# Storing a product's left matrix in column pairs, with one fewer place for gathered rows

## The chip, the cores and the metric

The kernel runs on one core of a Trainium2 chip. The metric is the device time of one execution in microseconds (us). Engines: PE is TensorE, DVE is VectorE, ACT is ScalarE, POOL is GpSimd, and SP only issues transfers here.

## The reference, cut to what matters

The program is two transformer-like blocks on 256 tokens of width 2048. The change touches the end of the second block, a layer in which every token picks 128 of 16384 experts:

```python
def block(args):                     # xt: 128 tokens, it: their 128 expert numbers, gt: weights
    xt, it, gt = args
    u = jnp.take(expert_u, it, axis=0)
    act = jax.nn.gelu(jnp.einsum('td,tkd->tk', xt, u)) * gt
    v = jnp.take(expert_v, it, axis=0)
    return jnp.einsum('tk,tkd->td', act, v)
```

The two blocks of 128 tokens are called t = 0 and t = 1. After this layer comes a residual sum and a final RMS norm.

## The kernel before

All engines walk one list of items that `Plan` writes; each engine executes, in the list's order, the items that it has a function for. The change concerns the last stage, which `dense` (from L1098) lists and which follows after everything else.

For the *lower* 1024 columns of the result, the rows of `expert_v` are not gathered. Before the stage, the activations of each token are scattered into a matrix over all 16384 experts, `A` (two halves, one for each t, in one tensor `AA`), built in 64 groups: PE makes a group in PSUM banks T0 or T1 (`build`, L1937), ACT copies it to SBUF (`keep_group`, L2426). The stage then multiplies `A` with the whole table: 128 tiles of 128 experts by 1024 columns. For tile j:

- SP copies the tile from HBM into `Vr` (L1609, 512 KB, five buffers, NT = 5). The copy for tile j waits until PE has finished tile j - 5.
- ACT rounds it to `Vh` (`high`, L2440, three buffers), and in the same function copies the tile's 2 x 128 columns of `AA` rounded into `Ah` (L2446, two buffers; the buffer is free when PE has finished tile j - 2).
- DVE makes the remainders, `Vl` in `low` (L3091) and `Al` in `low_a` (L3098).
- PE (`mul`, L1941) multiplies high by high, high by low and low by high in a fast format: 12 products of 512 columns, summed in the four banks W over all tiles. In 16 of the 128 tiles, those with j % 8 == 3, nothing is split: ACT copies the columns to `Ar`, and PE multiplies `Ar` and `Vr` whole.

For the *upper* 1024 columns the rows are gathered. Those of t = 0 were done earlier. Those of t = 1 (128), and 32 lower halves of t = 1 that the matrix leaves out, are the 160 *asides*: POOL gathers 128 half rows (512 KB) into one of five places `side` (L3224, NA = 5), and DVE multiplies by the activation and adds to `X` (`aside`, L3113). A gather into a place waits for the aside that used it before, NA earlier. Each aside on DVE also waits for the one ahead of it.

The order within a tile comes from `dense`: `high`, `low`, then one or two asides (160 over 120 tiles), then `low_a`, then `mul`. Four products on PE (`gain`, L1982) stand after tiles 7, 11, 15 and 19; at tile 22 ACT and DVE have a piece of the final norm (`upper`). DVE and ACT each take their instructions strictly in order, so whatever stands behind a waiting one waits too.

```python
a = 0
for j in range(128):
    self.add("high", j)
    self.add("low", j)
    if j == 0:
        self.add("rows")
    while a < min(ASIDES, (j - 1) * ASIDES // 120):
        self.add("aside", a)
        a += 1
    self.add("low_a", j)
    self.add("mul", j)
```

Of the kernel before, what the change touches and what calls it, by code (L numbers as in the profile page):

```python
# [7 lines left out]
F32 = mybir.dt.float32  # L8
F32R = mybir.dt.float32r
U32 = mybir.dt.uint32  # L10
ALU = mybir.AluOpType
ACT = mybir.ActivationFunctionType
AX = mybir.AxisListType.X
ADD, SUB, MUL = ALU.add, ALU.subtract, ALU.mult

P = 128
# [16 lines left out]
HALF = D // 2  # L33
# [4 lines left out]
FIRST_ROWS = 102  # L38
NT = 5
NH = 3  # L40
NA = 5
ASIDES = 128 + LATE
RAW = 8
NX = 5
U_SETS = ((48, (0, 1, 2, 3)), (190, (0, 1, 2, 3, 4, 5)), (218, (0, 2, 3, 4, 5)), (256, (2, 3, 4, 5)))
BACKLOG = {"ACT": 3.0, "DVE": 4.5, "DMA": 1e9}
# [104 lines left out]
def landings():  # L151

    count, table = [0] * NE, {}
    for kind, n, place in ("row", 128, row_sem), ("aside", ASIDES, lambda i: i % NA):
        for i in range(n):
# [22 lines left out]


def whole_tile(j):  # L180
    return j % RAW == 3


SPLIT_TILES = [j for j in range(128) if not whole_tile(j)]


def aside_of(i):
# [107 lines left out]
class Plan:  # L295
# [801 lines left out]
    def dense(self):  # L1097

        for i in range(ASIDES):
            self.add("get_aside", i)  # L1100
        a = 0
        for j in range(128):
            self.add("high", j)
            self.add("low", j)
            if j == 0:
                self.add("rows")
            while a < min(ASIDES, (j - 1) * ASIDES // 120):
                self.add("aside", a)
                a += 1
            self.add("low_a", j)  # L1110
            self.add("mul", j)
            if j % 4 == 3 and 7 <= j <= 19:
                self.add("gain", (j - 7) // 4)
            if j == 22:
                self.add("upper", 0)
        self.add("upper", 1)
        self.add("close")
# [77 lines left out]
def strided(a, *dims):  # L1195
    return bass.AP(tensor=a.tensor, offset=a.offset, ap=[list(a.ap[0])] + [list(d) for d in dims])


def program(nc, io, out):
    plan = Plan()  # L1200
    blocks, subs, chunks = plan.blocks, plan.subs, plan.chunks
    with ExitStack() as ctx:
        def sem(name):
            return ctx.enter_context(nc.semaphore(name))
# [3 lines left out]
        def at(name, shape, offset, dt=F32):  # L1208
            return nc.alloc_sbuf_tensor_at(name, [P] + list(shape), dt, offset=offset)
# [6 lines left out]
        class Area:  # L1216
# [17 lines left out]
        keep = low("keep", [2, T])  # L1234
# [22 lines left out]
        u0 = top[0]  # L1257
# [99 lines left out]
        A0_o, A1_o = 65280, 163808  # L1357
        AA = at("AA", [(END - A0_o) // 4], A0_o)
        A = [AA[:, o:o + P * P].rearrange("p (g k) -> p g k", k=4 * P) for o in (0, (A1_o - A0_o) // 4)]
# [39 lines left out]
        Vr = [at(f"Vr{i}", [HALF], o) for i, o in enumerate(tile_at)]  # L1399
        Vl = [at(f"Vl{i}", [HALF], o, F32R) for i, o in enumerate(tile_at)]  # L1400
        Vh = [at(f"Vh{i}", [HALF], o, F32R) for i, o in enumerate(high_at)]
        Ah = [at(f"Ah{i}", [2, P], u0 + 4096 + 2048 * i, F32R) for i in range(2)]
        Al = [at(f"Al{i}", [2, P], u0 + 5120 + 2048 * i, F32R) for i in range(2)]
        Ar = [at(f"Ar{i}", [2, P], u0 + 4096 + 2048 * i) for i in range(2)]
        side_place = [4, 4, 3, 3, 2]
        side_b = [at(f"side{i}", [HALF], o) for i, o in enumerate((u0 + 8192, u0 + 12288, u0 + 16384, u0 + 20480, u0))]

        halves_at = [raw0 + 8192 * (NR + i) for i in range(4)]
        place = [u0 + 8192, u0 + 24576, u0, u0 + 16384, Z + 8192]
# [11 lines left out]
        T0, T1, M0, M1 = (banks[n] for n in ("T0", "T1", "M0", "M1"))  # L1421
# [3 lines left out]
        s_whole = [sem(f"whole{i}") for i in range(8)]  # L1425
        s_hi, s_lo, s_taken = sem("hi"), sem("lo"), sem("taken")
# [61 lines left out]
        CK = [slice(512 * j, 512 * (j + 1)) for j in range(4)]  # L1488
# [137 lines left out]
        def tensor(q):  # L1626
            e = Once(q)
# [312 lines left out]
            def product(t, c, left, right, j, k):  # L1940
                return q.matmul(banks[f"W{2 * t + c}"][:, :], left, right, start=j == 0 and k == 0, stop=j == 127 and k == 2)  # L1941

            def mul(j):
                if j == 0:
                    e.wait_ge(s_dot, 256)
                a = j % 2
                e.wait_ge(s_whole[j % NT], 32 + 16 * (j // NT + 1))
                if whole_tile(j):
                    e.wait_ge(s_ah, j + 1)
                    for t in range(2):  # L1950
                        for c in range(2):
                            m = product(t, c, Ar[a][:, t, :], Vr[j % NT][:, CK[c]], j, 1)
                    m.then_inc(s_taken, 1)
                    return
                v = nth_split(j)
                e.wait_ge(s_lo, plan.split_subs + v)
                e.wait_ge(s_al, v)
                H, L = Vh[(v - 1) % NH], Vl[j % NT]
                if j == 127:
                    for t in range(2):  # L1960
                        for c in range(2):
                            product(t, c, Ah[a][:, t, :], H[:, CK[c]], j, 0)
                            product(t, c, Ah[a][:, t, :], L[:, CK[c]], j, 1)
                            product(t, c, Al[a][:, t, :], H[:, CK[c]], j, 2).then_inc(s_taken, 1)
                    return
                for t in range(2):
                    for c in range(2):
                        product(t, c, Ah[a][:, t, :], H[:, CK[c]], j, 0)
                    for c in range(2):
                        product(t, c, Ah[a][:, t, :], L[:, CK[c]], j, 1)  # L1970
                    for c in range(2):
                        m = product(t, c, Al[a][:, t, :], H[:, CK[c]], j, 2)
                m.then_inc(s_taken, 1)

            def gain(g):
# [18 lines left out]
        def scalar(q):  # L1994
            e = Once(q)
# [426 lines left out]
            def keep_group(i):  # L2422
                t, g = group_of(i)
                bank, _ = keeps(i)
                e.wait_ge(s_built, i + 1)
                q.activation(A[t][:, g, :].rearrange("p (k x) -> p k x", x=4),  # L2426
                             (T0, T1)[i % 2][:, :].rearrange("p (x k) -> p k x", x=4), ACT.Copy).then_inc(bank, 1)

            def high(j):
                a = j % 2  # L2430
                both = strided(AA[:, 4 * j:4 * j + 1], [(A1_o - A0_o) // 4, 2], [4 * P, 32], [1, 4])
                if not whole_tile(j):
                    v = nth_split(j)
                    e.wait_ge(s_whole[j % NT], 32 + 16 * (j // NT + 1))
                    if j == 0:
                        e.wait_ge(s_dot, 256)
                        e.wait_ge(s_built, 64)
                    if v > NH:
                        e.wait_ge(s_taken, len(subs) + SPLIT_TILES[v - NH - 1] + 1)
                    q.activation(Vh[(v - 1) % NH][:, :], Vr[j % NT][:, :], ACT.Copy).then_inc(s_hi, 1)  # L2440
                if j == 0:
                    e.wait_ge(*keeps(64))
                    e.wait_ge(*keeps(65))
                if j >= 2:
                    e.wait_ge(s_taken, len(subs) + j - 1)
                q.activation((Ar if whole_tile(j) else Ah)[a][:, :, :].rearrange("p t (g x) -> p t g x", x=4), both, ACT.Copy).then_inc(s_ah, 1)  # L2446

            def upper(t):
                if t:
# [12 lines left out]
            def close():  # L2462
# [16 lines left out]
                for t in range(2):  # L2479
# [10 lines left out]
                  "a_hi": a_hi, "turn_hi": turn_hi, "peer": peer, "turn_keys": turn_keys, "first_out": first_out, "first_keep": first_keep,  # L2490
                  "keep_scores": keep_scores,
                  "copy_xn": copy_xn, "top_exp": top_exp, "gelu": gelu, "spread": spread, "turn_ids": turn_ids, "turn_act": turn_act,
                  "one_hot": one_hot, "spike": spike, "keep": keep_group, "high": high, "upper": upper, "close": close})

        def vector(q):
            e = Once(q)
# [594 lines left out]
            def low_a(j):  # L3093
                if whole_tile(j):
                    return
                both = strided(AA[:, 4 * j:4 * j + 1], [(A1_o - A0_o) // 4, 2], [4 * P, 32], [1, 4])
                e.wait_ge(s_ah, j + 1)
                q.tensor_tensor(Al[j % 2][:, :, :].rearrange("p t (g x) -> p t g x", x=4), both,  # L3098
                                Ah[j % 2][:, :, :].bitcast(F32).rearrange("p t (g x) -> p t g x", x=4), SUB).then_inc(s_al, 1)

            def rows():
                e.wait_ge(s_spread, 128)
# [3 lines left out]
            def aside(i):  # L3106
# [154 lines left out]
```

## Time and profile before

| | |
|---|---|
| median of 3 runs (lowest, highest) | 3370.77 us (3370.76, 3371.5) |
| the profiled execution's own time | 3370.61 us |
| its span, first to last instruction | 3368.8 us |
| PE, DVE, ACT, POOL busy | 2976.6, 2600.1, 1692.1, 646.5 us |
| HBM read | 881.30 MB |

The profile belongs to one execution. Its span is 1.8 us shorter than that execution's time, which is 0.16 us under the median. "Busy" adds the spans of an engine's instructions; PE's ends are modelled. In tables of windows, the columns are the stretch, its length, the busy time of each engine with its count of instructions, the granted TensorE clock as a share of full speed, the mean busy share of the 16 DMA engines, and GB/s moved. The last stage runs from 2957 us to the end.

### The profile page before, as it was taken

The page shows a single profiled execution, that of the slowest core. Times are in us where ns is not written, and L with a number is a line of the kernel's source. Part 1 is how long each engine was busy: PE and PEld are TensorE (multiplying, and loading weights), DVE is VectorE, ACT ScalarE, POOL GpSimd, SP SyncE. Part 2 cuts the span into 40 slices and gives each one's busy share as a digit, 9 for nine tenths or more (in the row PEclk, how much of TensorE's full clock was granted, in tenths as well). Part 3 has the DMA queues.
Part 4 walks back from the last instruction along what each step waited for, and adds up shares of the span by engine and source line. Part 5 has one row for each costly group of instructions (what it writes and reads, how often), then busy time and mean ns, then how long its engine had stood idle before and what let it go on. Part 6 is the DMA issues. An engine that isn't in the chain of part 4 may idle for free. (4 is left out here: it accounts for less than half of the span.)

```text
span 3368.8 us, 37730 instructions
## 1 busy us (share of the span) xinstructions
PE 2976.6 (88%) x14064; PEld 2398.1 (71%) x14064; DVE 2600.1 (77%) x3915; ACT 1692.1 (50%) x2761; POOL 646.5 (19%) x565
## 2 busy tenths in 40 slices
PE   8999999999999999999999999986653543699998
PEld 7998998888888888888888888842211331566766
DVE  7786767775556878786557675799889887989997
ACT  6554556554445555554435763123434776644444
POOL 0000000000000000000000000555544334356663
PEclk9999999999999999999999999998876666589999
DMA  6554555555555555555556558999999999989997
GB/s 235 163 151 154 162 173 175 173 165 200 187 184 179 186 188 188 188 188 200 185 196 224 175 183 277 341 381 420 421 416 401 426 427 425 371 336 391 402 393 287
DMA packets 428952, 885.89 MB, mean 263 GB/s; under 512 B 19068, under 2 KB 249373, under 8 KB 395233
## 3 DMA queue, kind: packets, MB, share of 16 engines
q1 hardware_dynamic: 347208, 453.16, 40.3%
q0 software_dynamic: 80544, 429.95, 31.7%
q8 instruction: 112, 1.84, 0.2%
q14 instruction: 72, 0.58, 0.0%
q10 hardware_dynamic: 1016, 0.35, 0.0%
HBM read 881.30 MB, written 2.10 MB: 262 GB/s over the span
## 5 line engine op out<-in xcount | busy, mean ns | idle before, releaser
L2620 DVE TENSOR_TENSOR wl<-raw,wh 128x1024 fp32r<-128x1024 f32 (+1 forms) x720 | 850.9, 1187 | 563.0 <-ACT wh L2073 561.3
L2073 ACT ACTIVATE wh<-raw 128x1024 fp32r<-128x1024 f32 (+1 forms) x720 | 740.6, 1031 | 893.9 <-PE W L1777 573.1
L1767 PE MATMUL W<-u,wh 128*128 128x512 f32 x2040 | 722.6, 397 | 0.0
L1765 PE MATMUL W<-u,wl 128*128 128x256 f32 x2176 | 603.1, 282 | 0.2 <-DVE u L2582 0.2
L3061 DVE CUSTOM_DVE_ANT_0 Ub<-Ub,W 128x2048 f32<-128x2048 f32 x227 | 514.7, 2282 | 47.2 <-DMA Ub<-in_peer_u,ids 39.1
L1767 PEld LDWEIGHTS W<-u,wh 128*128 128x128 f32 x2040 | 383.3, 188 | 88.3
L1775 PE MATMUL W<-wh,u 128*128 128x512 f32 (+1 forms) x1152 | 436.2, 379 | 1.2 <-DVE u L2980 1.0
L1777 PE MATMUL W<-wh,u 128*128 128x512 f32 (+1 forms) x1152 | 427.9, 371 | 0.0
L1776 PE MATMUL W<-wl,u 128*128 128x512 f32 (+1 forms) x1152 | 427.6, 371 | 0.0
L1765 PEld LDWEIGHTS W<-u,wl 128*128 128x128 f32 x2176 | 410.8, 189 | 6.3 <-issue 0.5
L3197 POOL DMA_INDIRECT Ub<-in_peer_u,ids x256 | 263.9, 1031 | 413.2 <-DVE dots L3061 288.2
L1914 PE MATMUL M<-Vx,diag 128*128 128x512 f32 x360 | 188.1, 675 | 109.6 <-DMA Vx<-in_peer_v,vid 86.1
L1775 PEld LDWEIGHTS W<-wh,u 128*128 128x128 f32 x1152 | 216.5, 188 | 30.7 <-issue 1.4
L1777 PEld LDWEIGHTS W<-wh,u 128*128 128x128 f32 x1152 | 216.2, 188 | 30.6
L1776 PEld LDWEIGHTS W<-wl,u 128*128 128x128 f32 x1152 | 216.6, 188 | 29.0
L1914 PEld LDWEIGHTS M<-Vx,diag 128*128 128x128 f32 x360 | 73.7, 214 | 223.2 <-issue 175.6
L3224 POOL DMA_INDIRECT side<-in_peer_v,vid x128 | 194.1, 1516 | 114.7 <-DVE X L3113 94.2
L3113 DVE SCALAR_TENSOR_TENSOR X<-side,dots,X 128x1024 f32<-128x1024 f32 x160 | 205.0, 1281 | 5.2 <-DMA side<-in_peer_v,vid 0.6
L1914 PE MATMUL M<-Vy,diag 128*128 128x512 f32 x104 | 81.0, 935 | 133.6 <-DMA Vy<-in_peer_v,vid 108.4
L1937 PE MATMUL T<-spikes,AA 128*128 128x128 f32 (+1 forms) x512 | 116.1, 403 | 78.0 <-issue 58.4
L1937 PEld LDWEIGHTS T<-spikes,AA 128*128 128x128 f32 (+1 forms) x512 | 104.6, 302 | 97.8 <-issue 97.8
L1941 PE MATMUL W<-Vh,Ah 128*128 128x512 f32 x448 | 147.0, 409 | 26.7 <-DVE Al L3098 26.6
(401 smaller groups left out, 4840.5 us busy)
## 6 DMA issues: line engine op xcount, KB each, us to landing
raw<-in_w_in SPq DMA_DIRECT2D x128, 1024.0 KB, 5.2
raw<-in_w_up SPq DMA_DIRECT2D x88, 1024.0 KB, 4.8
Vr<-in_peer_v SPq DMA_DIRECT2D x128, 512.0 KB
raw<-in_w_down SPq DMA_DIRECT2D x44, 1024.0 KB, 5.0
raw<-in_w_in SPq DMA_DIRECT2D x144, 256.0 KB, 3.4
raw<-in_w_out SPq DMA_DIRECT2D x32, 1024.0 KB, 5.0
raw<-in_w_proj_a SPq DMA_DIRECT2D x16, 1024.0 KB, 5.0
Wb<-in_peer_w_q SPq DMA_DIRECT2D x16, 1024.0 KB, 6.7
```

What stands on the lines that cost most here:

```text
L1765: i = q.matmul(pr[h][:, 0:T], vl, xh, start=False, stop=False)
L1767: i = q.matmul(o, vh, u[:, :, kk, :], start=False, stop=last)
L1775: q.matmul(o, th, H[:, k, :], start=first, stop=False)
L1776: q.matmul(o, th, L[:, k, :], start=False, stop=False)
L1777: i = q.matmul(o, tl, H[:, k, :], start=False, stop=last)
L1914: i = q.matmul((M0, M1)[j][:, :], diag[:, m % 4, :], Vb[slot][:, CK[j]], start=m == 0, stop=m == 127)
L1937: m = q.matmul((T0, T1)[i % 2][:, col(x)], A[t][0:k, g, x * P:x * P + P], spikes[i % 2][0:k, x, :], start=True, stop=True)
L2073: q.activation(wh[:, s % NS, 0:b.half], r, ACT.Copy).then_inc(s_hi, 1)
L2620: q.tensor_tensor(wl[:, s % NS, 0:b.half], r, wh[:, s % NS, 0:b.half].bitcast(F32), SUB).then_inc(s_lo, 1)
L3061: q.tensor_tensor_reduce(U[:, :], U[:, :], inputs[:, :], 1.0, 0.0, MUL, ADD, dots[t][:, k:k + 1]).then_inc(s_dot, 1)
L3113: q.scalar_tensor_tensor(X[:, 1, c], side_b[i % NA][:, :], dots[1][:, k:k + 1], X[:, 1, c], MUL, ADD).then_inc(s_aside, 1)
L3197: q.indirect_dma_start(Ub[place][:, :], None, eu, bass.IndirectOffsetOnAxis(ids[t][:, k:k + 1], 0)).then_inc(s_u[place], 16)
```

## The change

Column pairs. Tiles 2p and 2p + 1 now share one buffer of twice the size: `high_a` (ACT) copies the columns for both tiles in one operation of 512 elements, and `low_a` (DVE) makes both remainders in one. Both run on even j only. The items are reordered: `high_a`, `high`, `low_a`, `low`, asides, `mul`. `AA` is stored so that the two columns of a pair are neighbours, which changes the pattern in which `keep_group` reads PSUM. PE reads a tile's left operand from the pair's buffer at every second element (8 bytes apart), where before it was contiguous.

Whole tiles. They are now the pairs j % 16 in (6, 7), still 16 of 128.

Places. The larger `Ah` and `Al` take the memory of the fifth `side`, so NA is 4. A pair's buffer is refilled when PE has finished tile 2p - 3.

```diff
-NA = 5
+NA = 4
 ASIDES = 128 + LATE
-RAW = 8
...
 def whole_tile(j):
-    return j % RAW == 3
+    return j % 16 in (6, 7)
...
         for j in range(128):
+            if j % 2 == 0:
+                self.add("high_a", j)
             self.add("high", j)
+            if j % 2 == 0:
+                self.add("low_a", j)
             self.add("low", j)
...
-            self.add("low_a", j)
             self.add("mul", j)
...
-        Ah = [at(f"Ah{i}", [2, P], u0 + 4096 + 2048 * i, F32R) for i in range(2)]
-        Al = [at(f"Al{i}", [2, P], u0 + 5120 + 2048 * i, F32R) for i in range(2)]
-        Ar = [at(f"Ar{i}", [2, P], u0 + 4096 + 2048 * i) for i in range(2)]
-        side_place = [4, 4, 3, 3, 2]
-        side_b = [at(f"side{i}", [HALF], o) for i, o in enumerate((u0 + 8192, u0 + 12288, u0 + 16384, u0 + 20480, u0))]
+        Ah = [at(f"Ah{i}", [2, P, 2], u0 + 4096 * i, F32R) for i in range(2)]
+        Al = [at(f"Al{i}", [2, P, 2], u0 + 2048 + 4096 * i, F32R) for i in range(2)]
+        Ar = [at(f"Ar{i}", [2, P, 2], u0 + 4096 * i) for i in range(2)]
+        side_place = [4, 4, 3, 3]
+        side_b = [at(f"side{i}", [HALF], o) for i, o in enumerate((u0 + 8192, u0 + 12288, u0 + 16384, u0 + 20480))]
...
-                    e.wait_ge(s_ah, j + 1)
+                    e.wait_ge(s_ah, j // 2 + 1)
...
-                e.wait_ge(s_al, v)
+                e.wait_ge(s_al, nth_pair(j) + 1)
...
-                        product(t, c, Ah[a][:, t, :], H[:, CK[c]], j, 0)
+                        product(t, c, Ah[a][:, t, :, k], H[:, CK[c]], j, 0)
...
-                q.activation(A[t][:, g, :].rearrange("p (k x) -> p k x", x=4),
-                             (T0, T1)[i % 2][:, :].rearrange("p (x k) -> p k x", x=4), ACT.Copy).then_inc(bank, 1)
+                q.activation(A[t][:, g, :].rearrange("p (k x s) -> p k x s", x=4, s=2),
+                             (T0, T1)[i % 2][:, :].rearrange("p (x k s) -> p k x s", x=4, s=2), ACT.Copy).then_inc(bank, 1)
...
+            def high_a(j):
+                p = j // 2
...
+                if p >= 2:
+                    e.wait_ge(s_taken, len(subs) + 2 * p - 2)
+                both = strided(AA[:, 4 * j:4 * j + 1], [(A1_o - A0_o) // 4, 2], [4 * P, 32], [1, 8])
+                q.activation((Ar if whole_tile(j) else Ah)[p % 2][:, :, :, :].rearrange("p t (g x) k -> p t g (x k)", x=4), both, ACT.Copy).then_inc(s_ah, 1)
```

On DVE, in the middle of the stage, this stood before (`Vl` is a tile's remainder, `X<-side` an aside, `Al` the remainder of the columns):

```order
L3091 TENSOR_TENSOR Vl_219<-Vr_214,Vh_222 128x1024
L3113 SCALAR_TENSOR_TENSOR X<-side_231,dots_191,X 128x1024
L3113 SCALAR_TENSOR_TENSOR X<-side_232,dots_191,X 128x1024
L3098 TENSOR_TENSOR Al_225<-AA,Ah_223 128x256
L3091 TENSOR_TENSOR Vl_215<-Vr_210,Vh_220 128x1024
L3113 SCALAR_TENSOR_TENSOR X<-side_233,dots_191,X 128x1024
L3098 TENSOR_TENSOR Al_226<-AA,Ah_224 128x256
```

And this stands there now, around a pair of whole tiles:

```order
L3111 TENSOR_TENSOR Al_225<-AA,Ah_223 128x512
L3103 TENSOR_TENSOR Vl_218<-Vr_213,Vh_220 128x1024
L3126 SCALAR_TENSOR_TENSOR X<-side_229,dots_191,X 128x1024
L3103 TENSOR_TENSOR Vl_219<-Vr_214,Vh_221 128x1024
L3126 SCALAR_TENSOR_TENSOR X<-side_230,dots_191,X 128x1024
L3126 SCALAR_TENSOR_TENSOR X<-side_231,dots_191,X 128x1024
L3126 SCALAR_TENSOR_TENSOR X<-side_232,dots_191,X 128x1024
L3126 SCALAR_TENSOR_TENSOR X<-side_229,dots_191,X 128x1024
L3111 TENSOR_TENSOR Al_225<-AA,Ah_223 128x512
L3103 TENSOR_TENSOR Vl_217<-Vr_212,Vh_222 128x1024
```

`Al` moved from behind a tile's asides to the front of the pair, and up to four asides now stand in a row, the fourth in the place that the first of them has just left.

On POOL, the first gathers of the stage with what they wait for, before (`aside` counts finished asides):

```order
L3224 DMA side_231<-in_peer_v,vid_195 128x1024 [waits dot]
L3224 DMA side_232<-in_peer_v,vid_195 128x1024
L3224 DMA side_233<-in_peer_v,vid_195 128x1024
L3224 DMA side_229<-in_peer_v,vid_195 128x1024 [waits aside]
L3224 DMA side_230<-in_peer_v,vid_195 128x1024 [waits aside]
```

and now:

```order
L3237 DMA side_231<-in_peer_v,vid_195 128x1024 [waits dot]
L3237 DMA side_232<-in_peer_v,vid_195 128x1024
L3237 DMA side_229<-in_peer_v,vid_195 128x1024 [waits aside]
L3237 DMA side_230<-in_peer_v,vid_195 128x1024 [waits aside]
L3237 DMA side_231<-in_peer_v,vid_195 128x1024 [waits aside]
```

The gathers wait for an aside one earlier in their row.

## Rows read from the trace of the kernel before

**Rows 1.** Busy time of the engines by stretches, columns as told above

```profile
2700.00:2800.00 100.00, 40.64 (x127) 27.51 (x125) 87.57 (x87) 77.77 (x217) 39.42 (x42) 0.59 1.01 427
...
2957.00:3337.00 380.00, 354.48 (x1400) 261.51 (x1400) 357.10 (x379) 162.80 (x237) 242.88 (x158) 0.99 0.99 385
3337.00:3369.00 32.00, 20.07 (x81) 14.95 (x80) 16.12 (x26) 13.57 (x28) 0.00 (x0) 0.88 0.33 118
```

**Rows 2.** The same view, inside the last stage

```profile
2957.00:3000.00 43.00, 37.86 (x139) 27.16 (x140) 35.98 (x41) 17.39 (x28) 24.75 (x17) 0.90 0.87 315
3000.00:3050.00 50.00, 47.24 (x186) 33.99 (x186) 46.61 (x50) 23.01 (x35) 27.78 (x20) 1.00 0.99 376
...
3100.00:3150.00 50.00, 46.96 (x187) 34.60 (x186) 48.25 (x51) 20.96 (x31) 32.40 (x22) 1.00 1.01 404
...
3200.00:3250.00 50.00, 46.69 (x189) 34.99 (x188) 47.41 (x52) 20.66 (x30) 33.74 (x23) 1.00 1.00 391
```

**Rows 3.** Who waited for whom in the last stage: us, times, longest us

```profile
POOL side L3224 <- DVE X L3113: 114.3, 112, 4.8
...
ACT Vh L2440 <- DMA Vr<-in_peer_v: 34.5, 48, 1.9
PE W L1941 <- DVE Al L3098: 26.6, 25, 4.6
...
DVE X L3113 <- DMA side<-in_peer_v,vid: 0.6, 2, 0.4
```

**Rows 4.** Groups of instructions in the last stage: count, busy us, mean ns, idle before

```profile
L3113 DVE SCALAR_TENSOR_TENSOR X<-side,dots,X 128x1024 f32<-128x1024 f32 x160 | 205.0, 1281 | 5.2 <-DMA side<-in_peer_v,vid 0.6 <-DMA side<-in_peer_v,vlow 0.3
L3224 POOL DMA_INDIRECT side<-in_peer_v,vid x126 | 192.2, 1525 | 109.4 <-DVE X L3113 94.2 <-issue 12.0 <-DVE dots L3061 3.3
...
L3091 DVE TENSOR_TENSOR Vl<-Vr,Vh 128x1024 fp32r<-128x1024 f32 x112 | 136.8, 1222 | 19.6 <-ACT Vh L2440 18.0 <-issue 1.1
L2440 ACT ACTIVATE Vh<-Vr 128x1024 fp32r<-128x1024 f32 x112 | 118.1, 1054 | 35.1 <-DMA Vr<-in_peer_v 34.5
L1941 PEld LDWEIGHTS W<-Vl,Ah 128*128 128x128 f32 x448 | 84.6, 189 | 18.5
...
L3098 DVE TENSOR_TENSOR Al<-AA,Ah 128x256 fp32r<-128x256 f32 x112 | 46.9, 418 | 4.6 <-ACT Ah L2446 4.5
L2446 ACT ACTIVATE Ah<-AA 128x256 fp32r<-128x256 f32 x112 | 46.7, 417 | 148.7 <-PE W L1941 143.5 <-issue 4.8
```

**Rows 5.** Instructions in order of time: start us, us, engine, idle before

```profile
3151.66 0.42 DVE L3098 TENSOR_TENSOR Al<-AA,Ah 128x256 fp32r<-128x256 f32 x1
...
3152.00 1.22 DVE L3091 TENSOR_TENSOR Vl<-Vr,Vh 128x1024 fp32r<-128x1024 f32 x1
3152.05 0.62 PE L1941 MATMUL W<-Vh,Al 128*128 128x512 f32 x2
...
3152.50 0.61 PE L1941 MATMUL W<-Vh,Ah 128*128 128x512 f32 x2
...
3153.13 1.28 DVE L3113 SCALAR_TENSOR_TENSOR X<-side,dots,X 128x1024 f32<-128x1024 f32 x1
...
3154.33 0.42 DVE L3098 TENSOR_TENSOR Al<-AA,Ah 128x256 fp32r<-128x256 f32 x1
```

**Rows 6.** The chain that ended last: tile copies from issue to landing (eight such)

```profile
3149.96 6.47 DMA Vr<-in_peer_v
...
3185.25 7.56 DMA Vr<-in_peer_v
```

**Rows 7.** One line's instructions, the copy of a built group from PSUM

```profile
L2426 ACT ACTIVATE AA<-T x64: 572/576/599, 2603.0 to 2956.8; 128x512 f32<-128x512 f32 x64
```

More of the change, by code:

```diff
@@ L180, in whole_tile, with nth_pair @@
 def whole_tile(j):
-    return j % RAW == 3
+    return j % 16 in (6, 7)
 SPLIT_TILES = [j for j in range(128) if not whole_tile(j)]
+SPLIT_PAIRS = [j // 2 for j in SPLIT_TILES if j % 2 == 0]
+def nth_pair(j):
+    return SPLIT_PAIRS.index(j // 2)
 def aside_of(i):
@@ L1945, in mul @@
                     e.wait_ge(s_dot, 256)
-                a = j % 2
                 e.wait_ge(s_whole[j % NT], 32 + 16 * (j // NT + 1))
+                a, k = j // 2 % 2, j % 2
                 if whole_tile(j):
-                    e.wait_ge(s_ah, j + 1)
+                    e.wait_ge(s_ah, j // 2 + 1)
                     for t in range(2):
                         for c in range(2):
-                            m = product(t, c, Ar[a][:, t, :], Vr[j % NT][:, CK[c]], j, 1)
+                            m = product(t, c, Ar[a][:, t, :, k], Vr[j % NT][:, CK[c]], j, 1)
                     m.then_inc(s_taken, 1)
@@ L1961, in mul @@
                         for c in range(2):
-                            product(t, c, Ah[a][:, t, :], H[:, CK[c]], j, 0)
-                            product(t, c, Ah[a][:, t, :], L[:, CK[c]], j, 1)
-                            product(t, c, Al[a][:, t, :], H[:, CK[c]], j, 2).then_inc(s_taken, 1)
+                            product(t, c, Ah[a][:, t, :, k], H[:, CK[c]], j, 0)
+                            product(t, c, Ah[a][:, t, :, k], L[:, CK[c]], j, 1)
+                            product(t, c, Al[a][:, t, :, k], H[:, CK[c]], j, 2).then_inc(s_taken, 1)
                     return
@@ L1967, in mul @@
                     for c in range(2):
-                        product(t, c, Ah[a][:, t, :], H[:, CK[c]], j, 0)
+                        product(t, c, Ah[a][:, t, :, k], H[:, CK[c]], j, 0)
                     for c in range(2):
-                        product(t, c, Ah[a][:, t, :], L[:, CK[c]], j, 1)
+                        product(t, c, Ah[a][:, t, :, k], L[:, CK[c]], j, 1)
                     for c in range(2):
-                        m = product(t, c, Al[a][:, t, :], H[:, CK[c]], j, 2)
+                        m = product(t, c, Al[a][:, t, :, k], H[:, CK[c]], j, 2)
                 m.then_inc(s_taken, 1)
@@ L2425, in keep_group @@
                 e.wait_ge(s_built, i + 1)
-                q.activation(A[t][:, g, :].rearrange("p (k x) -> p k x", x=4),
-                             (T0, T1)[i % 2][:, :].rearrange("p (x k) -> p k x", x=4), ACT.Copy).then_inc(bank, 1)
[L2429 to L2441, printed above, removed]
+                q.activation(A[t][:, g, :].rearrange("p (k x s) -> p k x s", x=4, s=2),
+                             (T0, T1)[i % 2][:, :].rearrange("p (x k s) -> p k x s", x=4, s=2), ACT.Copy).then_inc(bank, 1)
@@ L2442, in high @@
+            def high_a(j):
+                p = j // 2
+                if p == 0:
+                    e.wait_ge(s_dot, 256)
                     e.wait_ge(*keeps(64))
                     e.wait_ge(*keeps(65))
-                if j >= 2:
-                    e.wait_ge(s_taken, len(subs) + j - 1)
-                q.activation((Ar if whole_tile(j) else Ah)[a][:, :, :].rearrange("p t (g x) -> p t g x", x=4), both, ACT.Copy).then_inc(s_ah, 1)
+                if p >= 2:
+                    e.wait_ge(s_taken, len(subs) + 2 * p - 2)
+                both = strided(AA[:, 4 * j:4 * j + 1], [(A1_o - A0_o) // 4, 2], [4 * P, 32], [1, 8])
+                q.activation((Ar if whole_tile(j) else Ah)[p % 2][:, :, :, :].rearrange("p t (g x) k -> p t g (x k)", x=4), both, ACT.Copy).then_inc(s_ah, 1)
@@ new lines, in high @@
+            def high(j):
+                if whole_tile(j):
+                    return
+                v = nth_split(j)
+                e.wait_ge(s_whole[j % NT], 32 + 16 * (j // NT + 1))
+                if j == 0:
+                    e.wait_ge(s_dot, 256)
+                    e.wait_ge(s_built, 64)
+                if v > NH:
+                    e.wait_ge(s_taken, len(subs) + SPLIT_TILES[v - NH - 1] + 1)
+                q.activation(Vh[(v - 1) % NH][:, :], Vr[j % NT][:, :], ACT.Copy).then_inc(s_hi, 1)
@@ L2492, in scalar @@
                   "copy_xn": copy_xn, "top_exp": top_exp, "gelu": gelu, "spread": spread, "turn_ids": turn_ids, "turn_act": turn_act,
-                  "one_hot": one_hot, "spike": spike, "keep": keep_group, "high": high, "upper": upper, "close": close})
+                  "one_hot": one_hot, "spike": spike, "keep": keep_group, "high_a": high_a, "high": high, "upper": upper, "close": close})
         def vector(q):
@@ L3095, in low_a @@
                     return
[L3096 to L3099, printed above, removed]
+                p = j // 2
+                both = strided(AA[:, 4 * j:4 * j + 1], [(A1_o - A0_o) // 4, 2], [4 * P, 32], [1, 8])
+                e.wait_ge(s_ah, p + 1)
+                q.tensor_tensor(Al[p % 2][:, :, :, :].rearrange("p t (g x) k -> p t g (x k)", x=4), both,
+                                Ah[p % 2][:, :, :, :].bitcast(F32).rearrange("p t (g x) k -> p t g (x k)", x=4), SUB).then_inc(s_al, 1)
             def rows():
```

## The prediction

> **What bounds the kernel now.** I read the windows first. The diff touches two stages: the end of the build (one copy pattern) and the last stage, from 2957 us. The table of stretches shows three resources nearly full at once in that stage [rows 1]: over 380 us PE is busy 354 us, DVE 357 us, and the DMA engines 0.99, at 385 GB/s. Its last 32 us is a tail in which only tile copies and products remain. The finer stretches [rows 2] say which of the three is the limit: in the steady part the DMA share is 1.01 at 404 GB/s. Other traffic reached 427 GB/s [rows 1], but in that stretch longer rows are fetched too, so I take 404 as the limit for this mixture. Early in the stage the rate is only 315, then 376 GB/s: there DMA still has room.
>
> What must be moved: 160 asides and 124 tile copies (four tiles were there before), 284 transfers of 524288 bytes. One takes 0.524 MB / 404 GB/s = 1.30 us of all engines. The stretch of 380 us moved 385 x 0.380 = 146 MB, which at 404 would have needed 362 us. So **18 us is the most that any reordering can win** in it, and most of it lies in the first 93 us: 43 x (1 - 315/404) = 9.5 us and 50 x (1 - 376/404) = 3.5 us. The rest, about 5 us, is lost here and there (391 in one stretch).
>
> Next come the waits [rows 3]. ACT waits 48 times, 34.5 us, for a tile copy to land: copies are used as they arrive. PE waits for `Al` 25 times, 26.6 us, one of them the 4.6 us at the stage's start. DVE waits for a gather only 0.6 us: the five places are just enough. POOL waits 114.3 us for asides to free a place, which shows that each place is refilled the moment it can be.
>
> **The change, part by part**, against the profiled execution's 3370.6 us (the median of the runs is 3370.8, so the two can be used alike).
>
> *DVE's columns.* 112 operations of 418 ns go, 56 of 512 elements come. From 256 elements in 418 ns and 1024 in 1222 ns [rows 4] the slope is 1.05 ns an element, so 512 take about 686 ns, and the busy sum falls by 112 x 0.418 - 56 x 0.686 = 8.4 us. That overstates it: neighbours overlap. From the start of `Al` to the start of `Vl` is 0.34 us, and from `Vl` to the aside 1.13 us [rows 5]; by the same slope a pair costs 0.60 us against 2 x 0.34. DVE really gains 56 x 0.08 = about 4 us, over a stage in which DMA is the limit. By itself: 0.
>
> *ACT's columns.* 128 operations become 64; ACT is busy 163 of 380 us [rows 1]: 0. A pair's copy now waits for PE to finish tile 2p - 3 and stands ahead of that tile's `Vh`, but `Vh` has three buffers and for a run of split tiles waits for that same tile: nothing new queues behind it.
>
> *PE.* The same 112 split and 16 whole tiles, the same products. A pair of products takes 0.45 us [rows 5], a split tile 2.7 us, where DMA needs 2.33 transfers x 1.30 = 3.0 us a tile. PE has slack of about 0.3 us a tile.
>
> *The order.* `Al` no longer stands behind one or two asides of 1.28 us, so PE starts a tile when `Vl` is done. The 25 waits for `Al` go. What is late next is the landing of `Vr`: a shorter path from landing to product releases the buffer sooner, so the next copy is issued sooner, and DMA gets its work earlier. This pays where DMA is not full. The first product starts about 1 us earlier. Of the 13 us lost before 3050 us I take 5 (the slow start of PE, the four `gain` products and the piece at tile 22 stay), of the 5 us later 2. **Sum: -7 us**, ends 0 and -18.
>
> *The fifth place.* 160 asides go by in 380 us less the first few us, one per 2.34 us, so a place is used once in 5 x 2.34 = 11.7 us, and with four places once in 9.4 us. In it must fit the aside itself 1.28, POOL's issue 1.53 (mean of [rows 4]), some 0.3 us until POOL starts, and the flight. The profile gives no landings of gathers; the nearest rows are tile copies of the same size on the same engines, 6.5 to 7.6 us from issue to landing [rows 6]. Before: 11.7 - 3.1 = 8.6 us for a flight of 6.5 to 7.6: fits with 1 to 2 us to spare. Now: 6.3 us: short by 0.2 to 1.3 us each time round, 40 rounds, 8 to 50 us if flights stay as long. They will not: a flight of 7 us is worth 5.4 transfers of engine time, so it is mostly queueing, and one transfer less in the queue can shorten it by up to 1.3 us. Then the loss is 0. The low end is the likelier, since the engines stay full either way, but four asides in a row around each pair of whole tiles (8 such) meet only four places. I take 6 us of the 0 to 50. **Sum: +6 us.**
>
> *PE's left operand at every second element.* A weight load takes 189 ns [rows 4], and one is needed every 0.45 / 2 = 0.225 us [rows 5]. No row shows a strided load. Below: no change. I take no change, since a row of 189 ns for contiguous data leaves the load well away from the product's time; the other end is a rival below. The Trainium skill ("SBUF — State Buffer", under "Door 1") says that SBUF delivers full bandwidth when at least two accesses fall in one 16-byte line. Two fp32 values 8 bytes apart do just that, so by that rule the load stays as it is and the sum is the same; at any wider step it would speak against the change. No run here has shown it.
>
> *The build's copy from PSUM.* 64 copies of 576 ns [rows 7]; the count stays, the inner step changes from 128 elements to pairs. The price may go either way by some 0.1 us, and PE's next group waits for it in the last 32: -3 to +3 us, taken as 0.
>
> Sum: 3370.6 - 7 + 6 = 3369.6. I forecast **3370 us, no change that can be told**. A measurement of this kernel can tell about 0.2%, which is 6.7 us, from no change.
>
> **The rivals.**
>
> *Faster (0.20).* The queueing argument holds fully: with four places the flights shorten by what is missing, and the order's gain comes alone. For it: DMA is full at 1.01 whatever the number in flight, and DVE has 1 to 2 us to spare per aside. Against it: the spare is smaller than the 2.3 us that one place is worth. The time: 3370.6 minus 7 to 12 = 3359 to 3364, middle 3362.
>
> *Slower by the places (0.15).* Flights keep their length: a gather needs its fixed path and the slowest of 16 engines, and then DVE waits for the gather, in order, with `Vl` behind it; PE follows. It decides from the point at which a flight is longer than 6.3 us. At a shortage of 0.5 us in 40 rounds it costs 20 us, against 7 won: 3384. For it: all eight flights in the chain are above 6.3. Against it: they are tile copies, which are delayed by five gathers' traffic.
>
> *Slower by strided weights (0.05).* If a load takes twice as long, 378 ns, it exceeds the 225 ns between products: a split tile takes 12 x 0.378 = 4.5 us instead of 3.0, over 112 tiles +168 us: 3540. It decides from 250 ns a load, where PE's slack of 0.3 us a tile is used up.
>
> *Little change, the likeliest (0.60)*: 3370, own range 3363 to 3377.
>
> A version in which the change does less than it says I leave out: counts of whole tiles, products and bytes are equal, and both halves of the pairing are in the order of instructions.
>
> **How the numbers follow.** Range: from 3360 (all but the far end of the faster case) to 3381 (half of the slow case by places), leaving out about 2 in 10. Faster by over 0.2% takes the faster case and a small tail of the likeliest: 0.23. Slower by over 0.2%: both slow cases and a tail: 0.21. The rest, 0.56, is within 0.2%.
>
> **What the profile after should show.** Right: `Al` x56 at about 0.69 us, `Ah` x56 at about 0.63; PE's waits for `Al` gone, replaced by waits for `Vl`; DMA above 376 GB/s in the stretch 3000 to 3050; DVE now waiting some us for `side`, where it waited 0.6; weight loads at 189 ns. Wrong: `side` waits of over 15 us in sum (the places decide), or none with the stage 7 us shorter (the places were free), weight loads above 0.2 us, or the copy from PSUM away from 576 ns with the build's end moved from 2957 us.

## The result, and the profile after

The changed kernel takes **3389.8 us** (median of 5 runs, 3387.9 to 3393.4) where the kernel before took 3371.4 us in the same session (3370.8 to 3373.2). The ratio is 1.0055, with a 95% interval of 1.0044 to 1.0067: slower by 18.5 us, about three times what can be told from no change, and above the top of the range (3381). The profiled execution took 3393.0 us, its span is 3391.2 us.

The table of stretches of the changed kernel, columns as in [rows 1]:

```profile
2957.00:3337.00 380.00, 347.54 (x1330) 256.25 (x1330) 335.03 (x310) 144.23 (x170) 217.55 (x151) 0.98 0.97 364
3337.00:3392.00 55.00, 41.09 (x160) 30.42 (x158) 36.33 (x41) 20.13 (x33) 9.53 (x7) 0.94 0.60 224
2957.00:3000.00 43.00, 39.19 (x140) 29.06 (x140) 35.07 (x36) 17.01 (x22) 20.17 (x15) 0.87 0.82 292
3000.00:3050.00 50.00, 49.97 (x191) 36.22 (x190) 46.21 (x45) 22.05 (x27) 28.34 (x21) 1.00 1.00 385
3100.00:3150.00 50.00, 44.66 (x172) 32.59 (x171) 43.37 (x41) 17.55 (x20) 31.40 (x21) 1.00 0.97 357
3200.00:3250.00 50.00, 45.96 (x179) 33.82 (x177) 44.12 (x41) 17.77 (x20) 29.43 (x21) 1.00 0.98 367
```

The build's last copy ends at 2959.3 us, where it ended at 2957.4 before. That is no sign of the new copy pattern: kernels of the next section with the old pattern end it at 2956.3 to 2961.1 us. From the first `Vh` to the end the last stage takes 431.2 us instead of 411.4: its 19.8 us hold the loss. Set the rows against [rows 1, 2]. From 3000 to 3050 us the rate rose from 376 to 385 GB/s, as the forecast had it; in the steady part it fell from 404 to 357 and from 391 to 367. PE and DVE both do less in the same 50 us. The DMA share hardly moved (1.01 to 0.97, 1.00 to 0.98), so the share alone would not have told of a loss.

The chain of work that ended last, in the last stage, by its share of that stretch: the kernel before, then the changed one.

```profile
by line: PE W L1941 32.7%; DVE X L3113 23.2%; DMA Vr<-in_peer_v 13.7%; DVE Vl L3091 11.7%; issue 7.8%; ACT Vh L2440 3.0%; DVE Al L3098 2.0%; ACT squares L2471 0.7%; DVE X L3138 0.5%; PE T L1982 0.5%; PE M L1982 0.5%; ACT squares L2457 0.4%;
```

```profile
by line: DMA side<-in_peer_v,vid 36.1%; DVE X L3126 19.4%; issue 10.1%; DMA side<-in_peer_v,vlow 9.1%; DVE Vl L3103 7.5%; PE W L1949 7.5%; POOL side L3237 5.1%; ACT Vh L2458 0.7%; ACT squares L2483 0.7%; DVE X L3151 0.5%; PE T L1945 0.5%; D
```

Before, products, asides and tile copies take turns in it, and no gather is named. Now gathers are 45% of it (36.1 + 9.1).

Who waits for whom in the last stage of the changed kernel: us, times, longest us.

```profile
POOL side L3237 <- DVE X L3126: 155.0, 123, 7.5
...
ACT Vh L2458 <- DMA Vr<-in_peer_v: 63.8, 34, 3.0
ACT Vh L2458 <- PE W L1949: 54.6, 26, 4.7
DVE X L3126 <- DMA side<-in_peer_v,vid: 32.9, 35, 3.8
PE W L1949 <- DVE Vl L3103: 31.2, 30, 3.8
...
DVE X L3126 <- DMA side<-in_peer_v,vlow: 8.7, 8, 2.6
DVE Vl L3103 <- ACT Vh L2458: 4.7, 5, 1.6
```

DVE waits 41.6 us for gathers (32.9 + 8.7), where [rows 3] had 0.6 us for the first kind. PE's 26.6 us for `Al` have become 31.2 us for `Vl`: the wait has changed its name and not gone. ACT waits for tile copies 63.8 us, from 34.5. It also waits 54.6 us in 26 times with a `Vh` for PE, which [rows 4] did not show; its waits for PE with `Ah` fell from 143.5 to 125.5 us.

The groups of the same stage: count, busy us, mean ns, idle before.

```profile
L3126 DVE SCALAR_TENSOR_TENSOR X<-side,dots,X 128x1024 f32<-128x1024 f32 x160 | 205.4, 1284 | 45.2 <-DMA side<-in_peer_v,vid 32.9 <-DMA side<-in_peer_v,vlow 8.7
L3237 POOL DMA_INDIRECT side<-in_peer_v,vid x126 | 181.5, 1440 | 139.9 <-DVE X L3126 125.1 <-issue 11.5 <-DVE dots L3073 3.3
...
L3103 DVE TENSOR_TENSOR Vl<-Vr,Vh 128x1024 fp32r<-128x1024 f32 x112 | 136.4, 1218 | 4.8 <-ACT Vh L2458 4.7
...
L1949 PEld LDWEIGHTS W<-Vl,Ah 128*128 128x128 f32 x448 | 87.7, 196 | 17.6
...
L3111 DVE TENSOR_TENSOR Al<-AA,Ah 128x512 fp32r<-128x512 f32 x56 | 38.3, 684 | 1.8 <-ACT Ah L2446 1.8
L2446 ACT ACTIVATE Ah<-AA 128x512 fp32r<-128x512 f32 x56 | 35.3, 631 | 125.5 <-PE W L1949 125.5
```

Every duration is close to the one that was reckoned (684 ns for 686, 631 for about 630); the exception is the weight load, 196 ns for 189. No instruction's own cost explains 18 us. What grew on DVE is the idle time before `X`, from 5.2 to 45.2 us.

One place in order of time (start us, us, idle before in brackets) shows what such a wait does on an engine that works in order:

```profile
3141.19 2.70 DVE L3126 SCALAR_TENSOR_TENSOR X<-side,dots,X 128x1024 f32<-128x1024 f32 x2 [3.75 <-DMA side<-in_peer_v,vid]
...
3143.81 0.69 DVE L3111 TENSOR_TENSOR Al<-AA,Ah 128x512 fp32r<-128x512 f32 x1
...
3144.41 1.22 DVE L3103 TENSOR_TENSOR Vl<-Vr,Vh 128x1024 fp32r<-128x1024 f32 x1
...
3145.73 0.72 PE L1949 MATMUL W<-Vh,Ah 128*128 128x512 f32 x2 [0.87 <-DVE Vl L3103]
...
3155.33 1.06 ACT L2458 ACTIVATE Vh<-Vr 128x1024 fp32r<-128x1024 f32 x1 [2.12 <-DMA Vr<-in_peer_v]
```

DVE waits 3.75 us for the gather of the third of four asides in a row. `Vl` stands behind them and starts at 3144.4 us, though its `Vh` is ready at 3142.6, and PE stands idle 0.87 us for it. PE ends that tile at 3148.8 us; the copy that needed its `Vr` is issued at 3148.8 and lands at 3155.3, and ACT has waited 2.12 us for it. The lateness of a gather comes back as lateness of a copy.

### The profile page after: what moved, and what is told of

The parts are those of the page before. It is cut to its first block, busy times and chain, and to the rows that moved or that the text cites. A ratio compares the mean times of both kernels' runs of the same rounds, so it can differ in the third digit from the quotient of the medians.

```text
span 3391.2 us, 37649 instructions
## 1 busy us (share of the span) xinstructions
PE 2986.8 (88%) x14064; PEld 2404.5 (71%) x14064; DVE 2598.4 (77%) x3859; ACT 1680.2 (50%) x2697; POOL 628.9 (19%) x565
## 4 chain that ended last, share of the span: by engine, by line
PE 66%; DMA 17%; DVE 10%; issue 3%; POOL 2%; ACT 1%; DVEq 0%; SPq 0%; ACTq 0%; POOLq 0%
PE W L1775 14%; PE W L1783 11%; PE W L1785 11%; PE W L1784 11%; DMA Ub<-in_peer_u,ids 8%; PE W L1773 7%; DMA side<-in_peer_v,vid 5%; DVE Ub L3073 4%; DMA Vx<-in_peer_v,vid 3%; DVE X L3126 2%; PE M L1922 2%; PE T L1945 1%; PE M L1836 1%; PE W L1709 1%; DMA side<-in_peer_v,vlow 1%
## 5 line engine op out<-in xcount | busy, mean ns | idle before, releaser
L3126 DVE SCALAR_TENSOR_TENSOR X<-side,dots,X 128x1024 f32<-128x1024 f32 x160 | 205.4, 1284 | 45.2 <-DMA side<-in_peer_v,vid 32.9
L3237 POOL DMA_INDIRECT side<-in_peer_v,vid x128 | 183.3, 1432 | 145.1 <-DVE X L3126 125.1
L1945 PE MATMUL T<-spikes,AA 128*128 128x128 f32 (+1 forms) x512 | 109.2, 385 | 85.6 <-issue 62.9
L1949 PE MATMUL W<-Vh,Ah 128*128 128x512 f32 x448 | 147.6, 410 | 34.8 <-DVE Vl L3103 31.2
L2458 ACT ACTIVATE Vh<-Vr 128x1024 fp32r<-128x1024 f32 x112 | 117.9, 1054 | 118.4 <-DMA Vr<-in_peer_v 63.8
```

The costliest lines, as they stand in the source:

```text
L3237: q.indirect_dma_start(side_b[i % NA][:, :], None, ev_half, bass.IndirectOffsetOnAxis(index, 0)).then_inc(s_place[LANDS["aside", i][0]], 16)
```

## The experiments

In each, the ratio is to the kernel before on the same chip; its medians there were 3372.7, 3373.5 and 3373.2 us in the three sessions that follow. Kernels of different sessions are best compared by their ratios.

**Places alone.** The kernel before with four places and nothing else; then three.

```diff
-NA = 5
+NA = 4
...
-        side_place = [4, 4, 3, 3, 2]
+        side_place = [4, 4, 3, 3]
...
```

> The kernel before, with four places for gathered rows and nothing else changed. Places theory (the fifth place is what is lost): DVE waits for gathers 25 us or more in sum instead of 1, DMA falls from 404 to some 380 GB/s in the steady part, and the time rises by 12 to 25 us over before. Queueing theory (flights shorten by what is missing): within 3 us of before. PE theory (the strided weights of the changed kernel cost its time): no more than 5 us over before, since the weights are contiguous here.

> The kernel before with three places. With four places the flight of a gather, issue's end to landing, fell only from 6.7 to 6.0 us. Floor theory (a flight has a fixed length of about 5.5 to 6 us whatever is in the queue): one turn of a place stays at 5.7 + 3.8 us, three places give an aside per 3.2 us, and 160 of them cost about 130 us over before. Queueing theory (each place less shortens flights by 1.3 us, as the first step did not): 80 us or less over before.

Four places: 3390.3 us, ratio 1.0048 [1.0035, 1.0062]; three: 3465.2 us, 1.0273 [1.0257, 1.0289]. One place less, in an otherwise unchanged kernel, costs 17.6 us, which is nearly all of the change's 18.5; the next costs about 75 more. With three the time is 91.8 us over before, between the two cases that were put down (80 at most, or 130). Stretches of the one with four, then of the one with three:

```profile
3050.00:3300.00 250.00, 225.76 (x882) 164.97 (x881) 227.53 (x238) 99.92 (x145) 152.84 (x102) 0.99 0.99 377
```

```profile
3050.00:3300.00 250.00, 203.97 (x747) 146.22 (x746) 192.16 (x199) 80.51 (x121) 111.89 (x87) 0.95 0.88 316
```

The kernel before moved 400 GB/s in this stretch. And the waits with four:

```profile
PE W L1941 <- DVE Al L3098: 39.1, 31, 4.6
DVE X L3113 <- DMA side<-in_peer_v,vid: 20.6, 31, 2.2
...
DVE X L3113 <- DMA side<-in_peer_v,vlow: 6.8, 9, 1.8
```

DVE waits 27.4 us for gathers with nothing else changed, as was expected of the theory of places.

**The order alone.** `low_a` right behind `low` and ahead of the asides; with five places and with four.

```diff
             self.add("low", j)
+            self.add("low_a", j)
...
-            self.add("low_a", j)
             self.add("mul", j)
```

> The kernel before, with the remainder of the columns made directly behind the tile's remainder and ahead of the asides; five places, single tiles, contiguous columns. Order theory (my -7 us): 3 to 10 us under before, PE's waits for that remainder fall from 26.6 us to under 8, DMA above 376 GB/s in 3000 to 3050 us. Rival (DMA is the limit and the order is worth nothing): within 2 us of before.

> The same order with four places. If places and order add up, this is places4 plus what order5 wins. If the changed kernel's loss is the places alone, it lies within 4 us of the changed kernel (3390); if the strided weights or the pairs of whole tiles carry a part of the loss, it lies well under it, at 3375 to 3383.

With five places 3368.7 us, 0.9987 [0.9978, 0.9996]: a gain of 4 us, whose interval just leaves out 1. One expectation failed: PE's waits for `Al` did not fall under 8 us, as this kernel's waits say:

```profile
PE W L1941 <- DVE Al L3098: 21.9, 24, 3.4
```

Before, they were 26.6 us in 25 times. `Al` is now the last remainder that a tile's product needs, so a late `Vl` shows under its name. With four places 3393.2 us, 1.0058 [1.0045, 1.0072]: beside the 17.6 us of four places with the old order, no gain. In these two pairs of kernels the order is worth something only with five places. From 3000 to 3050 us the new order moves 388 GB/s with five places, but 358 with four; so the order alone does not explain the 385 of the changed kernel there. The kernel with four places and the new order has the changed kernel's order and places but single columns, and stands where that one does (1.0058 and 1.0055): the pairing itself moved nothing that can be measured.

**Every second element.** Four places and single columns, but written and read 8 bytes apart.

```diff
-        Ah = [at(f"Ah{i}", [2, P], u0 + 4096 + 2048 * i, F32R) for i in range(2)]
+        Ah = [at(f"Ah{i}", [2, P, 2], u0 + 4096 * i, F32R) for i in range(2)]
...
-                        product(t, c, Ah[a][:, t, :], H[:, CK[c]], j, 0)
+                        product(t, c, Ah[a][:, t, :, 0], H[:, CK[c]], j, 0)
```

> places4 with the columns of each tile written and read at every second element (8 bytes apart), one operation per tile as before. Stride theory: weight loads at 196 ns instead of 188, a split tile 2.80 us on PE instead of 2.72, and if PE's time counts in this stage, 128 x 0.08 = 10 us over places4, less if the slack of PE covers it. Rival: covered, within 3 us of places4. ACT's and DVE's operations on the columns keep 418 ns if the stride costs them nothing.

3393.4 us, 1.0059 [1.0045, 1.0072], 3.1 us above four places with contiguous columns; the two intervals overlap, so that cost is not shown. What is shown is the price of one load and of one copy, 196 and 439 ns for 189 and 417. Groups of this kernel:

```profile
L1941 PEld LDWEIGHTS W<-Vl,Ah 128*128 128x128 f32 x448 | 87.8, 196 | 18.0
...
L2446 ACT ACTIVATE Ah<-AA 128x256 fp32r<-128x256 f32 x112 | 49.2, 439 | 181.3 <-PE W L1941 181.3
```

**Bursts.** The changed kernel with its whole tiles back at j % 8 == 3, so that no four asides stand in a row around a pair of them. A pair with one whole tile is copied by two operations, one into `Ah` and one into `Ar`.

```diff
-    return j % 16 in (6, 7)
+    return j % 8 == 3
...
```

> The changed kernel with its 16 whole tiles where they were before, every eighth, so that never more than two or three asides stand in a row; columns in pairs, four places. Burst theory (asides four in a row find their places unfilled and cost time): 4 to 8 us under the changed kernel. Places theory: within 3 us of it, 17 to 21 us over before.

3391.5 us, 1.0052 [1.0038, 1.0065]. Nothing gained: the eight bursts are not where the time goes.

**Five places in the changed kernel.** The fifth takes the memory of `Vh`'s third buffer.

```diff
-NH = 3
-NA = 4
+NH = 2
+NA = 5
...
```

> The changed kernel with five places; the fifth takes the memory of the third buffer of the rounded tile (NH = 2). Places theory: nearly all of the loss of 18 us comes back, 3366 to 3376, less what two buffers instead of three cost (a few us). PE theory (strided weights and pairs carry the loss): stays above 3382.

3379.6 us, 1.0016 [1.0006, 1.0025]: each against the kernel before of its session, the loss falls from 18.5 to 6.2 us, between the two cases that were put down. The rest comes with a new wait:

```profile
ACT Vh L2458 <- PE W L1949: 177.4, 93, 5.6
...
PE W L1949 <- DVE Vl L3103: 25.1, 25, 3.8
...
DVE X L3126 <- DMA side<-in_peer_v,vid: 11.6, 11, 2.1
```

With two buffers `Vh` waits for PE 93 times (54.6 us in 26 times in the changed kernel). In this kernel PE leads the chain that ended last, with 46.5% of the stage's stretch, and gathers are 7%. So the strided weight loads may have a part in the rest, beside the two buffers; no run tells them apart. Three buffers, five places and pairs have no room together in this layout of the memory, so what the pairs would do with both was not tried.

**Spreading.** The asides over 124 tiles, not 120, in the new order with five places; this was meant as a better version.

```diff
-            while a < min(ASIDES, (j - 1) * ASIDES // 120):
+            while a < min(ASIDES, (j - 1) * ASIDES // 124):
```

> order5 with the 160 asides spread over 124 tiles instead of 120. If the bytes per us in the steady part are the limit, and the tail after the last aside runs on PE alone with DMA at half its rate, the steady part gets shorter by more than the tail grows: 2 to 5 us under order5. If gathers in flight, not bytes, are the limit, the asides' own time stays and it equals order5 or is 1 to 3 us slower.

**3356.8 us, 0.9951 [0.9937, 0.9964]**: 16.6 us faster than the kernel before, with five places and single columns, and 12 us under the new order alone, where 2 to 5 were expected. Its stretch and its waits:

```profile
3050.00:3300.00 250.00, 240.76 (x973) 181.29 (x973) 241.61 (x257) 110.97 (x158) 170.45 (x109) 1.00 1.02 404
```

```profile
PE W L1941 <- DVE Al L3098: 13.9, 18, 3.4
...
DVE X L3113 <- DMA side<-in_peer_v,vid: 4.8, 7, 1.1
```

Then the same edit in the changed kernel, in the kernel before (old order), in the paired one with five places; and 126 in the fastest.

> The changed kernel (four places, pairs) with its 160 asides spread over 124 tiles, not 120. The changed kernel took 3389.8 us. Theory (the ring of places sets the pace): a place turns in 9.8 us, so an aside comes every 2.45 us whatever the list says; the asides already fall behind the products, and a thinner list takes no wait away. 3386 to 3391 us, POOL's next release still bound to the aside, DVE still waiting 35 to 45 us for side. Rival (too much DVE work per tile sets the pace, and places only show it): the spreading that gave 12 us with five places gives as much here, 3378 us, and DVE waits under 30 us.

> The kernel before with nothing changed but the spreading, 124 instead of 120; five places, low_a still behind the asides. With both the new order and this spreading the time was 3356.8, with the order alone 3368.7, before 3371.4 to 3373.5. If the two gains are independent: 12 us less than before, about 3360. If the spreading pays only when the products do not wait for Al behind the asides: 3367 to 3371. PE's waits for Al (39 us with four places, 26.6 before) then stay above 22 us; with independent gains they fall too, since fewer tiles have two asides in front of low_a.

> The paired columns with five places (Vh has two buffers, which pays for the fifth) and the spreading over 124 tiles. With 120 it took 3379.6 us. If five places and the spreading are what matters: 3366 to 3370. If ACT's wait for a free Vh buffer (177 us in sum in the run with 120) is what held it: 3376 to 3380, no gain from the spreading.

> The fastest kernel so far (new order, five places, spreading 124: 3356.8 us), with the spreading over 126 tiles. If the gain of the spreading is linear in the asides per tile (1.33 to 1.29 gave 12 us; now 1.27): 3351 us. If its gain came from using the stage's empty tail, of which with 124 only some 17 us is left at a third of the rate: 3355 to 3359, because the last asides now stand behind the last tiles and the final norm waits for them.

| kernel | us | ratio to before |
|---|---|---|
| changed kernel, 124 | 3381.3 | 1.0026 [1.0016, 1.0036] |
| before, 124 | 3369.0 | 0.9992 [0.9983, 1.0001] |
| pairs, five places, 124 | 3376.3 | 1.0012 [1.0003, 1.0021] |
| new order, five places, 126 | 3358.1 | 0.9963 [0.9950, 0.9977] |

In three of the four the second of the two cases came: spreading pays little in the old order (its interval takes in 1, and PE's waits for `Al` stay at 23.7 us, where over 22 was expected), little in the paired kernel with two `Vh` buffers (its intervals with 120 and 124 overlap), and no more beyond 124. The changed kernel with 124 was put at 3386 to 3391 or at 3378 and landed between them, though DVE's wait for gathers (31.0 + 10.7 us) is where the theory of the ring of places had it. What that theory left out is the tail. The last asides, in the view of `X` from 3290 us on (count, then first and last start), of the changed kernel, of it with 124, and of the fastest kernel:

```profile
L3126 DVE SCALAR_TENSOR_TENSOR X<-side,dots,X x30: 1277/1284/1316, 3290.5 to 3360.3; 128x1024 f32<-128x1024 f32 x30
```

```profile
L3126 DVE SCALAR_TENSOR_TENSOR X<-side,dots,X x29: 1271/1284/1324, 3291.3 to 3361.1; 128x1024 f32<-128x1024 f32 x29
```

```profile
L3113 DVE SCALAR_TENSOR_TENSOR X<-side,dots,X x22: 1277/1280/1289, 3289.8 to 3337.3; 128x1024 f32<-128x1024 f32 x22
```

In the kernel before, the last aside starts at 3336.2 us. In the changed kernel it comes 24 us later (21.5 from the stage's start), whether the list is thick or thin; after it, PE still has to do the tiles that the list puts behind it. From each profiled execution (start of the stage taken as the first `Vh`; all in us):

| kernel | last aside done, from the stage's start | from there to the last tile's first product | from there to the end |
|---|---|---|---|
| before | 380.1 | 17.6 | 13.7 |
| before, 124 | 387.2 | 6.2 | 13.7 |
| new order, five places | 376.2 | 16.0 | 13.7 |
| the same, 124 | 379.1 | 4.5 | 13.7 |
| the same, 126 | 383.4 | -1.5 | 17.0 |
| four places alone | 400.4 | 17.6 | 13.7 |
| changed kernel | 401.6 | 15.9 | 13.7 |
| changed kernel, 124 | 405.0 | 4.7 | 13.7 |
| pairs, five places | 389.6 | 16.1 | 13.9 |
| the same, 124 | 397.9 | 4.7 | 13.6 |

The first column holds the price of the places (20 us for the fifth); the second is the tail that spreading takes away (11 us). With 126 the last aside ends 1.5 us after the last tile's first product has begun, and the last column grows from 13.7 to 17.0 us: the gain stops. Spreading alone, in the old order, shortens the tail by 11 us and delays the asides by 7; in the new order it delays them by 3. Together order and spreading give 16.6 us, where the medians give each alone about 4. That interaction is measured, in three sessions, each against the kernel before; why the old order delays its asides more was not tested beyond PE's waits for `Al`, 23.7 us there and 13.9 in the fastest kernel. In the paired kernel with five places the tail shrinks as well, but its asides go from 389.6 to 397.9 us, which fits `Vh`'s 175 us of waiting for PE, though no run gave it a third buffer.

## Why the prediction was wrong

**What bounds the kernel.** "I take 404 as the limit for this mixture" held over long stretches (the fastest kernel runs at 404 over 250 us, and none ran faster), though single slices below reach 420. What did not hold is the use made of it: "the engines stay full either way". Rates in 40 equal slices of the stretch from 3050 to 3300 us, with the packets, megabytes and share of each queue (q0 carries the gathers, q1 the tile copies). Before:

```profile
GB/s 411 399 414 420 403 373 391 414 420 405 418 389 360 411 418 412 414 374 397 420 421 381 419 412 381 401 412 383 341 418 410 381 418 389 419 377 361 405 418 400
...
q0 software_dynamic: 15659, 57.03, 57.7%
q1 hardware_dynamic: 11777, 42.87, 43.4%
```

And after:

```profile
GB/s 402 414 355 391 383 376 373 351 370 349 397 317 366 379 366 315 394 413 349 396 344 366 369 340 391 341 381 368 356 409 389 303 392 340 323 395 411 368 400 385
...
q0 software_dynamic: 14564, 53.05, 57.1%
q1 hardware_dynamic: 10838, 39.43, 41.2%
```

Before, dips below 360 are one in 40 slices; after, 13 in 40. On average fewer transfers are under way: from the end of a gather's or a tile copy's issue to its landing, 4.9 before, 4.4 in the changed kernel and 5.2 in the fastest one. But slice by slice the count does not tell where the dips are (4.3 in the changed kernel's 13 slow slices, 4.4 in its others), so what makes a single dip stays open.

**The fifth place, "+6 us", is the step that failed.** Its size was about 20: 17.6 us between medians when done alone, 20.3 us in the table above. The sum of the ring was right in form. Over asides 10 to 149, with the landing taken as the last event of the gather's semaphore before the aside starts (mean us):

| | aside | POOL starts | issue | flight | landing to use | ring |
|---|---|---|---|---|---|---|
| before | 1.28 | 0.54 | 1.56 | 6.67 | 1.59 | 11.64 |
| four places alone | 1.28 | 0.48 | 1.52 | 6.02 | 0.51 | 9.81 |
| changed | 1.28 | 0.47 | 1.45 | 6.19 | 0.48 | 9.87 |
| three places | 1.28 | 0.41 | 1.26 | 5.31 | 0.46 | 8.72 |

Two things went wrong in it. "One transfer less in the queue can shorten it by up to 1.3 us": it shortens it by 0.65, and by 0.71 for the next one. So a gather gives back only half of what a transfer costs the engines, and the argument of "mostly queueing" does not carry the loss down to nothing. And the point of decision, "longer than 6.3 us", was compared with a mean. To keep the old pace of one aside in 2.33 us, four places may turn in 9.31 us, which leaves 9.31 - 1.28 - 0.48 - 1.52 = 6.03 us for flight and rest together. The mean flight is 6.02. It would fit only if every gather landed at the very moment of its turn; but flights go from 5.0 to 7.4 us (tenth and ninetieth percentile), and an aside can't be taken before its turn. So 0.51 us stays between landing and use, and 0.51 x 40 rounds is 20 us. Before, 6% of the asides began within 0.1 us of their landing; with four places 36%, with the change 39%.

**The order, "-7 us".** Right in direction and too large in size: 4 us with five places, where the early stretch did rise above 376 GB/s. With four places no gain was measured. I added the two terms as if they were independent; the runs fit a gain that lives on the spare time that the lost place took away. "The 25 waits for `Al` go" held in name only: in the changed kernel waits for `Vl` stand in their place, at 31.2 us longer than what went, and with the order alone 21.9 us of them stay.

**The 18 us as "the most that any reordering can win"** was said of the stretch of 380 us alone, and the last 32 us of the stage, which [rows 1] show at 118 GB/s, got no term. The fastest kernel wins 16.6 us, most of it there: its tail is 13 us shorter. I had the row and did not use it.

**The rivals.** Slower by the places (0.15, 3384) was the nearest: right in its place and chain of waits, with "0.5 us in 40 rounds costs 20 us" nearly to the digit. That digit was luck, since 0.5 us was an assumed value between 0.2 and 1.3, and its premise failed: flights did not keep their length, and their mean of 6.02 us lies under its "longer than 6.3 us". The 7 us of gain set against it did not come. Its chance was too low, because the flights that spoke for it were set aside for a queueing argument that no row had shown. The faster case fell with the same argument. Strided weights fell too. "Nothing new queues behind it", of ACT, was wrong by the 54.6 us that `Vh` now waits for PE; single columns with the same order and places show no such wait and take the same time, so it cost nothing that can be told.

**Right:** DVE's and ACT's durations and their zero effect, as far as measured (single columns with the same order and places take the same time). The copy from PSUM, which answers to [rows 7] in the changed kernel:

```profile
L2434 ACT ACTIVATE AA<-T x64: 571/576/598, 2604.3 to 2958.7; 128x512 f32<-128x512 f32 x64
```

**Weight loads** at 189 ns were wrong by a little: 196 ns, in the changed kernel and with the stride alone. The Trainium skill ("SBUF — State Buffer", under "Door 1") promises full bandwidth for two accesses in one 16-byte line; here the loads are 4% longer, so the measurement decides, and the rule holds only nearly. What it makes of the time is not resolved: 3 us between two medians whose intervals overlap.

## What to carry to other kernels

Before you take a buffer away from a ring, write its turn as a sum (use, release, issue, flight, and the time from landing to use) and ask what is left of the last term. With in-order engines it needs room for the scatter of the flights, here 1.6 us were there before, and a third of it was not enough (nothing between was tried); a mean that just fits is already a loss. A DMA share near 1 does not say that bytes are at their ceiling: compare GB/s with the best stretch of the same mixture. And look at where two interleaved streams end: the one that finishes early leaves a tail of the other that one number in the list can fill.

## What the runs showed of the hardware that I had not expected

- The DMA engines' busy share stays at 0.99 to 1.02 while the rate goes from 404 to 371 GB/s. Share per megabyte in the rows above, from 3050 to 3300 us: gathers 57.7 / 57.03 = 1.01 before and 57.1 / 53.05 = 1.08 after, tile copies 1.01 and 1.04. With four places alone the two are 1.04 and 1.07, with three 1.12 and 1.11. So a packet occupies its engine longer in the kernels with fewer places, which have fewer transfers under way; why was not tried.
- A gather's issue on POOL takes from 0.93 to 2.3 us (once 3.2, in the fastest kernel), and its mean falls as places go: 1.56, 1.52 and 1.26 us with five, four and three. Why was not tried.
- A copy on ACT into every second element took 439 ns for 417, with DVE's at 420 for 418.
